# Three transformer-style layers on one core: 512-column matmuls for the gate and up pairs, another layout of bank pairs, a head in quarters, sums over 128 columns

## The reference

```python
# layer 1: attention over chunks, beside a gated linear recurrence, then a gated feed-forward part
u = rmsnorm(h, norm_mix_g) @ w_in                  # q, k, v, xr, gr, ga, gb
ya = chunked_band_attention(q, k, v, rel_table) @ w_attn_out
yb = (rg_lru(causal_depthwise_conv(xr)) * gelu(gr)) @ w_rnn_out
h = h + (sigmoid(ga + b) * ya + sigmoid(gb + b) * yb) @ w_o
g, up = split(rmsnorm(h, norm_ffn_g) @ w_ffn_in)   # 2 x 2816 columns
h = h + (silu(g) * up) @ w_ffn_out
h = rmsnorm(h, final_norm_g)
# layer 2: gated delta rule (8 heads of 128), then an MLP of 4096 hidden columns
# layer 3: causal attention with ALiBi (8 heads of 128), then an MLP of 4096
h = h + relu(rmsnorm(h) @ w_up) ** 2 @ w_down      # the MLP of layers 2 and 3
```

## Time and profile before

| | |
|---|---|
| median of 3 runs | 1193.99 us (1193.93 to 1196.65) |
| the profiled execution | 1196.81 us |
| its span, first to last instruction | 1195.1 us |
| TensorE busy | 1144.0 us (96%) |
| VectorE, ScalarE, POOL busy | 752.3, 564.9, 219.7 us |
| mean granted TensorE clock | 0.984 |

### The profile page before, as it was taken

The page is one execution under the profiler, slowest core; times in us unless marked ns, Lnnn a source line. Parts: engine busy times, 40 slices in busy tenths (PEclk is TensorE's granted clock), DMA queues, the critical chain, the costliest instruction groups (busy, mean ns, idle before and its releaser), DMA issues.

```text
span 1195.1 us, 21847 instructions
## 1 busy us (share of the span) xinstructions
PE 1144.0 (96%) x8900; PEld 1106.9 (93%) x8900; DVE 752.3 (63%) x913; ACT 564.9 (47%) x721; POOL 219.7 (18%) x226
## 2 busy tenths in 40 slices
PE   4999899999999999998999999999989999999997
PEld 4999789999999999998999998889989999888996
DVE  3745975576566543589968567763366757776433
ACT  4546456535454343456635355543344445554331
POOL 4895001502000000246373020000030002000001
PEclk9999999999999999899899999999999999999999
DMA  9654443655555555345420056555535445565541
GB/s 259 225 175 142 141 141 108 199 167 164 176 196 190 177 177 179 103 140 177 137 76 2 9 176 199 181 177 186 188 118 191 163 139 178 179 197 187 175 140 36
DMA packets 154852, 187.34 MB, mean 157 GB/s; under 512 B 6400, under 2 KB 143776, under 8 KB 154784
## 3 DMA queue, kind: packets, MB, share of 16 engines
q1 hardware_dynamic: 149072, 183.51, 47.3%
q10 hardware_dynamic: 5712, 2.86, 0.9%
HBM read 185.29 MB, written 1.07 MB: 156 GB/s over the span
## 4 chain that ended last, share of the span: by engine, by line
PE 86%; DVE 9%; issue 2%; ACT 2%; DMA 1%; POOL 0%; SPq 0%; DVEq 0%; POOLq 0%; ACTq 0%
PE PS L332 20%; PE PS L333 19%; PE PS L334 19%; PE PS L388 10%; PE PS L390 5%; DVE WL L328 2%; DVE XHL L485 1%; PE PS L397 1%; PE PS L396 1%; PE PS L395 1%; ACT WH L319 1%; PE PS L1798 1%; DMA RAW<-in_w_in 1%; PE PS L1784 1%; PE PS L677 1%
## 5 line engine op out<-in xcount | busy, mean ns | idle before, releaser
L328 DVE TENSOR_TENSOR WL<-RAW,WH 128x2048 fp32r<-128x2048 f32 x173 | 409.2, 2366 | 251.8 <-ACT WH L319 251.8
L319 ACT ACTIVATE WH<-RAW 128x2048 fp32r<-128x2048 f32 x173 | 330.0, 1909 | 251.3 <-PE PS L334 203.1
L332 PE MATMUL PS<-XHL,WH 128*128 128x256 f32 x1184 | 346.9, 293 | 27.3 <-DVE WL L328 18.8
L333 PE MATMUL PS<-XHL,WH 128*128 128x256 f32 x1184 | 340.5, 288 | 0.0
L334 PE MATMUL PS<-XHL,WL 128*128 128x256 f32 x1184 | 340.2, 287 | 0.0
L332 PEld LDWEIGHTS PS<-XHL,WH 128*128 128x128 f32 x1184 | 233.2, 197 | 33.1 <-DVE WL L328 18.4
L333 PEld LDWEIGHTS PS<-XHL,WH 128*128 128x128 f32 x1184 | 233.2, 197 | 0.3
L334 PEld LDWEIGHTS PS<-XHL,WL 128*128 128x128 f32 x1184 | 232.7, 197 | 0.0
L332 PE MATMUL PS<-HH,WH 128*128 (+1 forms) x688 | 195.0, 283 | 4.3 <-DVE SG L1581 2.8
L333 PE MATMUL PS<-HL,WH 128*128 (+1 forms) x688 | 194.7, 283 | 0.0
L334 PE MATMUL PS<-HH,WL 128*128 (+1 forms) x688 | 194.7, 283 | 0.0
(11 more groups left out here) (287 smaller groups left out, 1538.3 us busy)
## 6 DMA issues: line engine op xcount, KB each, us to landing
RAW<-in_mlp_w_up SPq DMA_DIRECT2D x32, 1024.0 KB, 5.5
RAW<-in_mlp_w_down SPq DMA_DIRECT2D x32, 1024.0 KB, 4.9
RAW<-in_w_in SPq DMA_DIRECT2D x28, 1024.0 KB, 5.2
RAW<-in_w_ffn_in_pairs SPq DMA_DIRECT2D x22, 1024.0 KB, 5.1
RAW<-in_dn_w_in SPq DMA_DIRECT2D x16, 1024.0 KB, 5.7
RAW<-in_mb_w_in SPq DMA_DIRECT2D x12, 1024.0 KB, 5.2
RAW<-in_w_ffn_out SPq DMA_DIRECT2D x11, 1024.0 KB, 5.0
RAW<-in_w_attn_out SPq DMA_DIRECT2D x4, 1024.0 KB, 5.1
```

What stands on the lines that cost most here:

```text
L319: act.activation(WH[:, k], RAW[:, k], ACT.Copy).then_inc(hi_done, 1)
L328: dve.tensor_tensor(WL[:, k], RAW[:, k], WH[:, k].bitcast(F32), ALU.subtract).then_inc(lo_done, 1)
L332: pe.matmul(out, wh, xh, start=start, stop=False, skip_group_check=True)
L333: pe.matmul(out, wh, xl, start=False, stop=False, skip_group_check=True)
```

## The change

Segment fi gets wide matmuls: `times_x` becomes `times_x_wide`, ScalarE copies the low halves of every chunk to SG (`low_half`), VectorE adds the high halves (`add_halves`) and works on from SG. The bank pairs become (4, 2, 6), and fo, w0 and w1 wait only for the last chunk whose pair lies in banks 0 to 3. In the head, x and the first two weight chunks come, are split and are multiplied in quarters; the additions of squares move to VectorE; ScalarE loads a table ahead; the sums and transposes of norm 0 come one half chunk later; the gate weights are issued by SP; the small inputs and the bias table are issued later; the softplus on VectorE is begun early and finished in qk0. The small sums of norms and of the delta rule, with 1, 2 or 16 columns, are made with 128 columns, each later one written over the surplus of the one before.

```diff
+        def piece_of(c, p):
+            return (slice(None), c, slice(512 * p, 512 * p + 512))
+        def piece_landed(c, p):
+            return piece_in[3 * c + p] if p < 3 else raw_in[c]
+        def fetch_piece(eng, c, p):
+            dst = RAW[piece_of(c, p)].rearrange("p (k n) -> p k n", k=2)
+            eng.dma_start(dst, source("xr", c)[:, 2 * p:2 * p + 2, :]).then_inc(piece_landed(c, p), 16)
+        def split_hi_piece(act, c, p):
+            act.wait_ge(piece_landed(c, p), 16)
+            act.activation(WH[piece_of(c, p)], RAW[piece_of(c, p)], ACT.Copy).then_inc(s_.hi_piece if p < 3 else hi_done, 1)
+        def split_lo_piece(dve, c, p):
+            if p < 3:
+                dve.wait_ge(s_.hi_piece, 3 * c + p + 1)
+            else:
+                dve.wait_ge(hi_done, c + 1)
+            dve.tensor_tensor(WL[piece_of(c, p)], RAW[piece_of(c, p)], WH[piece_of(c, p)].bitcast(F32),
+                              ALU.subtract).then_inc(s_.lo_piece if p < 3 else lo_done, 1)
+        def multiply_pieces(pe, st):
+            c = st.base
+            h = WH[:, c].rearrange("p (k n) -> p k n", k=KB)
+            l = WL[:, c].rearrange("p (k n) -> p k n", k=KB)
+            for p in range(4):
+                if c == 0:
+                    pe.wait_ge(s_.xl_ready, p + 1)
+                if p < 3:
+                    pe.wait_ge(s_.lo_piece, 3 * c + p + 1)
+                else:
+                    pe.wait_ge(lo_done, c + 1)
+                for b in range(2):
+                    part = slice(b * P, b * P + P)
+                    for k in (2 * p, 2 * p + 1):
+                        mm = product(pe, PS[:, c, b * TOK:(b + 1) * TOK], h[:, k, part], l[:, k, part], XH[:, k], XL[:, k],
+                                     k == 0 and b == 0, k == KB - 1)
+            mm.then_inc(mm_done, 1)
...
-        WIDE = (3, 5, 1)
+        WIDE = (4, 2, 6)
...
-        def banks_free(pe, sg):
-            for k in range(SLOTS):
-                pe.wait_ge(freed[k], uses_upto(sg, k) - sum(1 for c in range(sg.first, sg.first + sg.n) if c % SLOTS == k))
+        def rows_banks_free(pe, wide):
+            c = max(wide.first + j for j in range(wide.n) if WIDE[j % SLOTS] < 4)
+            pe.wait_ge(freed[c % SLOTS], c // SLOTS + 1)
...
-        SUMS_AT = [2, 2, 1, 2, 2, 2]
-        ROWS_AT = [3, 3, 2, 5, 3, 5]
+        SUMS_AT = [3, 2, 1, 2, 2, 2]
+        ROWS_AT = [4, 3, 2, 5, 3, 5]
...
-            return 0 if m in (3, 5) else 4
+            return 0 if m in (1, 3, 5) else 4
...
-            return 7 if m in (3, 5) else 5
+            return 1 if m in (1, 3, 5) else 5
...
-                        mm = pe.matmul(PS[:, 4, 2 * c:2 * c + 2], XN[:, j, c * P:(c + 1) * P], W2[:, j],
-                                       start=(j == 0), stop=(j == KB - 1))
+                        mm = pe.matmul(PS[:, 4, 2 * c:2 * c + P].rearrange("p (r e) -> p r e", e=2), XN[:, j, c * P:(c + 1) * P],
+                                       W2[:, j, None, :].to_broadcast([P, P // 2, 2]), start=(j == 0), stop=(j == KB - 1))
...
-                    mm = pe.matmul(PS[:, sums_bank(m), c:c + 1], XN[:, 0, c * P:(c + 1) * P], ONES[:, 0:1], start=True, stop=True)
+                    mm = pe.matmul(PS[:, sums_bank(m), c:c + P], XN[:, 0, c * P:(c + 1) * P], ONES[:], start=True, stop=True)
...
-            for name, n in SEGMENTS:
-                steps(sp, seg[name], lambda st: fetch(sp, st), head=SLOTS if name == "xr" else 0)
+                fetch_piece(sp, 0, p)
+            for p in range(4):
+                fetch_piece(sp, 1, p)
+            fetch(sp, Step(seg["xr"], 2, None))
+            sp.wait_ge(s_.ext_ready, 1)
+            sp.dma_start(ext_dram, EXT[:]).then_inc(s_.ext_out, 16)
...
+            for r, w in enumerate(("w_rg_r", "w_rg_i")):
+                for e in range(2):
+                    sp.dma_start(WRI[64 * e:64 * e + 64, r, :, 64 * e:64 * e + 64],
+                                 a[w].rearrange("(j e) d f -> e d j f", e=2)[e]).then_inc(s_.wri_in, 16)
+            fetch(sp, Step(seg["xr"], 3, None))
+            for name, n in SEGMENTS[1:]:
+                steps(sp, seg[name], lambda st: fetch(sp, st))
...
-            pool.tensor_tensor(WBA[:], WBA[:], G23[:, :, None].to_broadcast([P, KB, 16]), ALU.mult).then_inc(s_.prep, 1)
-            norm_add(pool, pc, 0)
...
+        def low_half(act, st):
+            act.wait_ge(mm_done, st.count())
+            act.activation(two(SG[:, st.slot]), wide_sides(st)[1], ACT.Copy).then_inc(s_.low_out, 1)
+        def add_halves(dve, st, earlier):
+            dve.wait_ge(s_.low_out, st.local(earlier))
+            dve.tensor_tensor(two(SG[:, st.slot]), two(SG[:, st.slot]), wide_sides(st)[0], ALU.add).then_inc(freed[st.slot], 1)
...
-            act.dma_start(AROW[:], a["dn_a_log"].partition_broadcast(P)).then_inc(s_.row_in, 16)
-            act.dma_start(DTB[:], a["dn_dt_bias"].partition_broadcast(P)).then_inc(s_.row_in, 16)
-            act.dma_start(WBA[:], cols(a["dn_w_in"], 4096, 16)).then_inc(s_.row_in, 16)
+            act.wait_ge(s_.const, 1)
+            act.activation(SUM[:, 0:1], EPSC[:], ACT.Exp)
             act.wait_ge(s_.vec_in, 16)
-            first = Step(seg["xr"], 0, None)
             for p in range(4):
                 norm_high(act, 0, p, squares=False)
-            split_hi(act, first, 0)
+                split_hi_piece(act, 0, p)
+            squares(act, 0, 0)
+            squares(act, 0, 1)
+            act.wait_ge(s_.ey_done, 1)
+            act.activation(SMALL[:, 1, 0:8], SMALL[:, 1, 0:8], ACT.Exp, scale=-1.0).then_inc(s_.sm_ready, 1)
             for p in range(4):
-                squares(act, 0, p)
-            split_hi(act, first, 1)
-            act.wait_ge(s_.wri_zero, 1)
-            act.wait_ge(s_.pool, 2)
-            for r, w in enumerate(("w_rg_r", "w_rg_i")):
-                for e in range(2):
-                    act.dma_start(WRI[64 * e:64 * e + 64, r, :, 64 * e:64 * e + 64],
-                                  a[w].rearrange("(j e) d f -> e d j f", e=2)[e]).then_inc(s_.wri_in, 16)
-            act.wait_ge(s_.ext_ready, 1)
-            act.dma_start(ext_dram, EXT[:]).then_inc(s_.ext_out, 16)
-            act.wait_ge(s_.ext_out, 16)
-            act.dma_start(BIAS[:], bass.AP(tensor=ext_dram.tensor, offset=0, ap=[[1, P], [384, 16], [1, TOK]])).then_inc(s_.bias_in, 16)
+                split_hi_piece(act, 1, p)
+            squares(act, 0, 2)
+            squares(act, 0, 3)
+            def late_inputs():
+                act.dma_start(AROW[:], a["dn_a_log"].partition_broadcast(P)).then_inc(s_.row_in, 16)
+                act.dma_start(DTB[:], a["dn_dt_bias"].partition_broadcast(P)).then_inc(s_.row_in, 16)
+                act.dma_start(WBA[:], cols(a["dn_w_in"], 4096, 16)).then_inc(s_.row_in, 16)
+                act.wait_ge(s_.ext_out, 16)
+                act.dma_start(BIAS[:], bass.AP(tensor=ext_dram.tensor, offset=0, ap=[[1, P], [384, 16], [1, TOK]])).then_inc(s_.bias_in, 16)
...
-                    act.wait_ge(s_.const, 1)
+                if st.j == 1:
                     norm_root(act, 0)
-                if st.j == 2:
-                    act.wait_ge(s_.ey_done, 1)
-                    act.activation(SMALL[:, 1, 0:8], SMALL[:, 1, 0:8], ACT.Exp, scale=-1.0).then_inc(s_.sm_ready, 1)
...
+                if st.j == 2:
+                    late_inputs()
+                if st.j == 0:
+                    act.wait_ge(s_.sp_ready, 1)
...
+                low_half(act, st)
                 if st.i is not None or st.j:
-                    silu_ready(act, st)
+                    squares_ready(0)(act, st)
...
+            lam = vec_at["rg_lambda"]
+            ch(dve.tensor_scalar(SMALL[:, 0, 0:8], VEC[:, lam:lam + 8], -1.0, None, ALU.mult))
+            softplus_start(8)
             for p in range(4):
                 norm_low(dve, 0, p)
-            split_lo(dve, first, 0)
-            split_lo(dve, first, 1)
+                split_lo_piece(dve, 0, p)
+            for p in range(4):
+                split_lo_piece(dve, 1, p)
+            dve.wait_ge(s_.sq_done, 4)
+            ch(dve.tensor_tensor(XN[:, 0:4], XN[:, 0:4], XN[:, 4:8], ALU.add))
+            ch.wait(dve)
+            ch(dve.tensor_tensor(XN[:, 0:2], XN[:, 0:2], XN[:, 2:4], ALU.add))
+            ch.wait(dve)
+            dve.tensor_tensor(XN[:, 0], XN[:, 0], XN[:, 1], ALU.add).then_inc(s_.sq_added, 1)
...
-                    ch(dve.tensor_scalar(NSP8[:], sp, -8.0, None, ALU.mult))
-            for st in (Step(seg["qk"], j, None) for j in range(8)):
-                split_lo(dve, st)
+                    dve.tensor_scalar(NSP8[:], sp, -8.0, None, ALU.mult).then_inc(s_.sp_ready, 1)
+                    ch.wait(dve)
                 dve.wait_ge(mm_done, st.count())
...
-                dve.tensor_tensor(SG[:, st.slot, 0:TOK], PS[:, st.slot, 0:TOK], RSTD[:], ALU.mult).then_inc(s_.sg_in, 1)
+                add_halves(dve, st, 0)
+                dve.wait_ge(freed[st.slot], st.uses())
```

(24 more changed lines are left out.)

51 lines of the change are left out of this document (26 added, 25 removed).

## The result

The changed kernel takes 1181.75 us (median of 4 runs, 1180.99 to 1183.01), the kernel before 1193.96 us (4 runs, 1193.92 to 1196.65): ratio 0.9893, interval [0.9876, 0.9910], 12.2 us faster. Forecast were 1175.3 us, with 1167 to 1185 as range. The profiled execution took 1181.85 us around a span of 1180.1; before it was 1196.81 around 1195.1. So the two traces lie 15.0 us apart.

The account below looks back on a forecast made before the run. TensorE, working nearly all the time, was taken as the bound. Head −8.5, fi and fo +2.3, banks −3.3 and sums −9.2 make −18.7 us: 1196.8 to 1178.1, less 2.8 to the median, 1175.3 us; range 1167 to 1185.

Parts of the forecast that it names:

- Head: Start of the kernel: quartered first chunks let TensorE start near 7 us and end qk0 at 42.6, −8.5 us.
- qk0 read near 43: Sign for the head: VectorE reads qk0 near 43 us, where it read it at 51.36 before.
- the late root: Head: ScalarE comes to the first norm's root only behind the split of xr3; 1 us of waiting put there.
- Wide matmuls in fi: Segment fi with the fo boundary: VectorE's add makes the cycle 5.94 us, TensorE's gain turns into idle time, +2.3 us.
- wide pays: Rival in fi: the ScalarE and VectorE cycle is not the bound, fi gives −6.5, 1166.5 us; chance 0.09.
- slower: Rival in fi: TensorE, idle 0.39 us in every chunk, loses its clock; eleven of 22 chunks make 1232 us; chance 0.03.
- The fo boundary: From fi to fo: fo1's weights ready at 427.7, fo0 ends at 427.1, so another 0.6 us of waiting.
- about 1 us each before fo0 and fo1: Sign at the start of fo: TensorE idle about 1 us before each of its first two chunks.
- Banks: u0 and u1: pairs (4, 2, 6) remove TensorE's idle time before w0 and w1, −3.3 us.
- Full sums: Small sums in dq, dz and at 675.10: 128 columns cost nothing more and keep the clock up, −9.2 us.
- From the profiled run to the median: Whole kernel: the median of runs, 1194.0, lies 2.8 us below the profiled run, so 1178.1 becomes 1175.3 us.

Follow-up runs that it names:

- experiment 3: Changed kernel, but in fi VectorE adds the halves and multiplies by the row factors before the low part of the weights: 1176.32 us.
- experiment 1: Changed kernel with only segment fi put back to 256-column matmuls and fo waiting for all three of its banks: 1175.11 us.
- 6: Changed kernel with everything in the head taken back to the kernel before, on all queues and engines: 1190.34 us.
- 9: Changed kernel with root and reciprocal of the first norm ahead of the split of the fourth chunk's weights: 1179.24 us.
- Experiment 2: Changed kernel with the weights of the second chunk of fo split ahead of the last gate pair, not behind it: 1179.78 us.
- Experiment 4: The kernel before, unchanged, profiled once more as its second profile: 1194.06 us in one run.
- experiment 5: Changed kernel with all its sums back to outputs of 1, 2 or 16 columns a matmul: 1187.64 us.
- 7: Changed kernel with bank pairs (3, 5, 1) in u0 and u1 and w0 and w1 waiting for all three slots: 1185.20 us.
- experiment 8: Changed kernel with fi's VectorE order changed from the fourth chunk on, the fo1 split ahead of the last gate, and the first norm's root and reciprocal earlier: 1172.36 us.
- 10: Changed kernel with fi back to 256-column matmuls and the first norm's root and reciprocal earlier: 1175.11 us.

## Why the prediction was right and where it was off

*Head.* −8.5 forecast, −8.85 measured to the end of wo, +8.6 when taken back alone. First matmul at 6.82 (near 7 said). The first chunk of qk ended 1.4 us earlier than forecast (41.2 for 42.6), but the sign "qk0 read near 43" failed: VectorE read it at 45.13, behind the softplus chain, at no cost to TensorE. The wait for the late root was priced at 1 us and was 1.77, in other runs 2.83 with a slow clock behind; what was gained above that went partly into a longer stretch ahead of gr0.

*Wide matmuls in fi.* The claim that TensorE's gain turns into idle time, with a cycle of 5.94 us, holds: 5.95 measured, and 5.55 when the order on VectorE is changed (3). The rival *wide pays* falls with experiment 1. The clock stood at 1.00 from 121.4 to 421.7 in spite of the short wait in every chunk of fi, so *slower* falls as well. The Trainium skill, page "TensorE: Matmul & The Clock Gate", section "A second HAM failure mode: psum-queue depth-cycling", has small pauses between groups of matmuls make the clock swing; these 300 us do not show it.

*The fo boundary: the step that failed.* "fi21 runs from 415.4 to 421.0; behind it come copy, add, SG, silu with hh, WH and WL for fo1 ... another 0.6 us of waiting." It let the last chain start when TensorE ends fi21. But here, where ScalarE and VectorE bound the segment, they were a chunk behind: when TensorE ended fi21, the gate of fi20 had still to be added, and both gate pairs went ahead of the split. TensorE waited 2.68 us, and then lost some 1.5 us to the clock (fi and fo take 198.48 with that stretch and 196.96 to 196.98 without, in 6 and 9). By rows the 4.5 us are: 0.5 in fi (fo0 starts 131.26 us behind the last addition of wo, 2.35 more than before, where 1.9 were forecast), 2.4 from fo0 to fo1 (8.67 us, where 6.3 were forecast; 2.1 of it is the wait), and 1.6 behind that, 1.5 of it the clock. The sign "about 1 us each before fo0 and fo1" failed at both: nothing and 2.68. Experiment 2, which only moves the split, gave 3.2 of the 4.5 us back.

*Banks.* −3.3 forecast, −3.4 by the trace, 3.45 when taken back.

*Full sums.* −9.2 forecast, −9.5 in the two traces, of which 1.0 is not the sums' but the longer half clock behind the pause ahead of dq11 in the first profile (4); that the two agree so closely is in part luck. The mechanism is shown by 5. The size was read from one profiled run that had long stretches; against the second profile it is 125.72 − 120.24 + 0.9 = 6.4 us, and taking the sums back cost 5.9.

*From the profiled run to the median: the second step that failed.* "The median of the runs is 1194.0, 2.8 us lower, so 1175.3 us is forecast." The subtraction took it that the profiled run's 2.8 us lie outside of what changes. Experiment 4 shows them in the half-clock stretches of dq and dz: some 2 us in the very ones that the term of 9.2 takes its gain from, 1 us at dq11, where the changed kernel's run drew the short form. The gain was to be counted either from a usual run (6.4) or from the profiled one (9.2), and then at most the 1 us of dq11 was to be taken off besides. The traces lie 3.7 us less apart than forecast (4.5 at fo, less 0.8 that the other rows gave beyond the forecast), and with the 2.8 us here that is the miss of 6.45 us. It is a third of the forecast gain; the measured time lies within the range, which is 18 us wide, and the two errors went the same way.

## What to carry to other kernels

Before a matmul is made cheaper at the price of more work on the engines that feed it, draw their cycle and look what stands in it: here an add of 0.7 us made the cycle the bound, and another order on one engine took the 2.2 us of WL out of it without any work saved. Where such a cycle bounds a segment, look how far behind the engines end it: here it was one whole chunk, and what the next segment needed from them waited for all of that. When a term is read from one profiled run, ask whether that run's distance to the median lies in the very stretch that the change removes.

## What the runs showed of the hardware

What the clock does after a pause of TensorE differs from run to run. The same wait of 2.7 us ahead of fo1 was followed by 3.4 to 3.5 us at half clock in the changed kernel and in experiments 5 and 7, and by none in experiments 6 and 9; the pause ahead of dq11 by 3.4, 6.8 or 0 us. A stretch of 3.4 us costs up to 1.7 and can cost nothing: dq and dz take 120.24 us with one behind the pause ahead of dq11 (changed kernel), 120.26 without (1), and 121.34 with 6.8 us (10). In the two profiles of the kernel before, stretches at the same places and of other lengths make the 2.8 us between them.

Groups of fp32 matmuls with 1 to 16 output columns, issued back to back, were met by half clock in all three profiles that have them, at five groups of five in both of the kernel before and at four of five in experiment 5; they take 3.63 us for 32 matmuls of one column, against 3.74 with 128 columns. In the nine profiles with 128 columns no such stretch was seen at them. But do is not safe for that: experiments 1 and 10 have 3.4 us at half clock from 661.2 and 661.5, behind the 2.0 us wait ahead of do, where the changed kernel has none behind the same wait.

The same wide matmuls ran at two steady paces, 5.55 us for a chunk in fi of experiment 3 and 5.64 in fi of experiment 8, at full clock and without waits. No run here tells why.
